# Sparse softmax in a hybrid attention block: copies of turned probabilities moved ahead of the exponentials, and the first two score products without their wait

## The chip, the cores and the metric

The kernel runs on one core of a Trainium2 chip. Its time is the device time of one execution in microseconds (us), the median of three runs. The engines are named as the profile names them: PE is TensorE (PEld its weight loads), DVE is VectorE, ACT is ScalarE, POOL is GpSimd, and SP is the queue that issues the loads.

## The reference

Two layers of a block with three attention branches over 512 positions, 8 heads each: a stick-breaking branch, a latent branch ("mla", a causal softmax), and a sparse branch ("dsa"). The change lies in the sparse branch and at the border before it. Cut to what matters:

```python
def dsa_attention(q, k, v, ix_q, ix_k, ix_w, positions, rel_bias):
    ...
    _, sel = lax.top_k(score, topk)              # 128 keys of each query
    ...
    logits = jnp.einsum('bqhd,bqkd->bqhk', qb, kg) * (dh ** -0.5)
    bias = rel_bias.astype(jnp.float32)[t5_bucket(pq[:, :, None] - pk)]
    logits = logits + jnp.moveaxis(bias, -1, 2)
    p = jax.nn.softmax(jnp.where(valid[:, :, None, :], logits, -jnp.inf), axis=-1)
    return jnp.einsum('bqhk,bqkd->bqhd', p, vg)
```

The gates, an up projection for each branch and an output projection come after the three branches, and then the next layer.

## The kernel before, in words

Each engine has one program, written by hand in the order in which the engine works through it. Engines wait for each other on counting semaphores (`wait_ge`), and a wait holds up all that stands behind it on the same engine. So two things set what runs when: the written order and the waits.

**Units and steps.** A softmax unit is one head and one tile `t` of 128 queries. Its scores are 128 x w with w = 128(t+1), since later keys are masked. There are 32 units of the mla branch (u = 0 to 31, `N_MLA` = 32) and 32 of the sparse branch (u = 32 to 63). The sparse ones are taken in pairs: step j (0 to 15, `DSA_STEPS` = 16) has the units 32+2j and 33+2j, which are two heads (o = 0, 1) at the same t = j mod 4. So the widths go 128, 256, 384, 512 and begin again, four steps make a pair of heads, and there are four such rounds.

**What a unit goes through.** In the text, S, X and so on are these operations, with the line numbers of the kernel before:
- S: PE multiplies queries and keys into one of the banks 0 to 3 (L1018, `s_of`); X: PE adds the mask to it (L1025, `chosen_of`).
- M: DVE adds the bias and takes the row maximum, into the buffer `probs[u % 4]` (L1874); N: DVE negates the maximum (L1878).
- E: ACT takes the exponentials in place, with their sum (L1435, `exp_of`).
- I: DVE inverts the sum (L1829, `inverse`); then POOL scales the row, "norm" below (L2019).
- T: PE transposes the row in t+1 pieces into one of two banks, 4 and 5 (L1037, `t_of`).
- C: ACT copies it out of the bank into `probs_dsa[u % 4]` (L1481).
- V: PE multiplies it with the values into bank 7 (L1066, `values_of`). Every fourth step ACT copies that bank out (L1441, `pair_out`).

**The order in a step j.** PE: S of both units of j, X of both, T of the units of step j-2 (`DSA_T` = 2), V of step j-3 (`DSA_AV` = 3). DVE: M and N of both units of j, then both I. ACT: E of both units of j, then C of both units of j-2. POOL follows the I.

**The waits that matter.** S(u) waits for N(u-4), since the bank is used again. M(u) waits for X(u) and for T(u-4), since `probs` has four buffers. T(u) waits for norm(u) and for C(u-2), since there are two banks. V waits for both C of its step. For the first four sparse units S waits instead for an exponential of the mla branch (L998).

**Work that goes along.** Two slabs of weights for the next stage are split in halves into a rounded part and a rest: ACT does the first behind its step 3, 5, 7 and 9 (L631), DVE the second behind its step 4, 6, 8 and 10 (L637). At j = 16 and 17 PE runs the two halves of the first projection of the next stage, `z0_0` (L736 to L738), between the last transposes. In the steps 0 to 2 the last mla units are still finished (`mla_tail`, L1053).

Of the kernel before, what the change touches and what calls it, by code (L numbers as in the profile page):

```python
# [31 lines left out]
P = 128  # L32
# [102 lines left out]
N_MLA = N_SOFT // 2  # L135
DSA_STEPS = N_MLA // 2
DSA_T, DSA_AV = 2, 3
# [52 lines left out]
def build(nc, x, positions, norm_g, w_in, q_norm_g, kv_norm_g, w_uq, w_ukv, mla_q_g, mla_k_g,  # L190
# [4 lines left out]
    with ctx:  # L195
        def signal(name):
            signals[name] = Signal(ctx.enter_context(nc.semaphore(name)), name, known, layer)
            return signals[name]
# [93 lines left out]
        soft = [soft3[:, 0, :], soft3[:, 1, :], soft3[:, 2, :], soft4[:, :]]  # L292
# [82 lines left out]
        pv_done = signal("pv_done")  # L375
# [3 lines left out]
        probs_exp = signal("probs_exp")  # L379
        row_inv = signal("row_inv")  # L380
        probs_normed = signal("probs_normed")
        probs_turned = signal("probs_turned")
        probs_t_ready = {br: signal(f"probs_t_ready_{br}") for br in ("mla", "dsa")}
# [68 lines left out]
        def dsa_units(j):  # L452

            return [(N_MLA + 2 * j + o, o, 2 * (j // ST) + o, j % ST) for o in range(2)]
# [169 lines left out]
        def split_hi(e, name, part=None):  # L624

            s, n = SLAB_NO[name], slab_size(name)
            a, b = (0, n) if part is None else (part * n // 2, (part + 1) * n // 2)
            if not part:
                e.wait_ge(*raw_in[s % RAW].at(name))
                wait_ring_slot(e, name)  # L630
            e.copy(w_hi[:, s % RING, a:b], raw[:, s % RAW, a:b]).then_inc(*hi_ready.tick(name, part or 0))  # L631
# [12 lines left out]
        def s_bank(u):  # L644
            return bank[2 + u % S_RING] if u < N_MLA else bank[(u - N_MLA) % 4]

        def t_bank(u):
            return bank[2 + S_RING + u % T_RING]

        def turned(u):  # L650

            br, h, t = soft_units[u]
            w = P * (t + 1)
            if br == "dsa":
                return probs_dsa[:, u % 4, 0:w]
            if h % 2 == 0:
                return probs_even[:, OFF[t]:OFF[t] + w]
            return probs_odd[:, (u // (2 * ST) * ST + t) % ODD, 0:w]

        def turned_before(u):  # L660

            br, h, t = soft_units[u]
            if br == "dsa":
                return u - 4 if u >= N_MLA + 4 else N_MLA - 1
            if h % 2 == 0:
                return u - ST if u >= ST else None
            n = u // (2 * ST) * ST + t - ODD
            return n // ST * 2 * ST + ST + n % ST if n >= 0 else None
# [14 lines left out]
        def _(pe):  # L683
# [30 lines left out]
            for layer.l in range(DEPTH):  # L714
# [275 lines left out]
                def s_of(u):  # L990

                    br, h, t = soft_units[u]
                    b, w = s_bank(u), P * (t + 1)
                    q = slice(t * P, (t + 1) * P)
                    if u >= N_MLA + 4:
                        pe.wait_ge(*row_max.at(u - 4))
                    elif u >= N_MLA:
                        pe.wait_ge(*probs_exp.at(N_MLA - 1 if u % 2 else N_MLA - 2))  # L998
                    elif u >= S_RING:
                        pe.wait_ge(*probs_exp.at(u - S_RING))  # L1000
                    else:
                        pe.wait_ge(*stick_prob.at(N_STICK - 1))
                    if br == "mla":
                        if t == 0:


                            pe.wait_ge(*dve_evac.at(f"qh{h}rope"))
                            pe.wait_ge(*pool_work.at(f"kh{h}rope"))
                            pe.wait_ge(*dve_evac.at(f"kh{h}"))
                        pe.matmul(b[:, 0:w], q_head[:, h % 2, q], k_head[:, h % 2, 0:w], start=True, stop=True)  # L1010
                        mm = pe.matmul(b[:, w - P:w], big_eye[:, :], causal[:, :], start=False, stop=True, skip_group_check=True)
                        mm.then_inc(*logits.tick(u))
                    else:
                        if h == 0 and t == 0:
                            pe.wait_ge(*dve_evac.at("ds_q3"))
                            pe.wait_ge(*topk.at("chosen", ST - 1))
                        r = slice(HD * (h % 2), HD * (h % 2) + HD)
                        pe.matmul(b[:, 0:w], ds_q[r, h // 2, q], ds_k[r, 0:w], start=True, stop=True)  # L1018
# [59 lines left out]
                for i in range(N_MLA):  # L1078
                    s_of(i)
                    if i in (1, 2):  # L1080
                        values_b(i + 1)
                    br, h, t = soft_units[i]
                    if h + 1 < HEADS:
                        if t == 0:
                            prep_k(h + 1)
                        if t == 2 and h + 2 < HEADS:
                            prep_q(h + 2)
                    if i >= T_LAG:
                        t_of(i - T_LAG)
                    if h + 1 < HEADS:  # L1090
                        if i == 0:
                            norm_q(1)
                        if t == 1:
                            norm_k(h + 1)
                        if t == 3 and h + 2 < HEADS:
                            norm_q(h + 2)
                    if i >= AV_LAG and soft_units[i - AV_LAG][1] % 2:
                        av_of(i - AV_LAG)
# [77 lines left out]
        def _(e):  # L1176
# [66 lines left out]
            for layer.l in range(DEPTH):  # L1243
# [184 lines left out]
                def exp_of(u):  # L1428
                    br, h, t = soft_units[u]
                    w = P * (t + 1)  # L1430
                    e.wait_ge(*row_max.at(u))
                    if br == "mla" and u >= PR:
                        e.wait_ge(*probs_turned.at(u - PR))
                    dst = probs[:, u % PR, 0:w]
                    e.activation(dst, s_bank(u)[:, 0:w] if br == "mla" else dst, ACT.Exp, bias=stat[:, 16 + u % 4:17 + u % 4],  # L1435
                                 accum_out=stat[:, 20 + u % 4:21 + u % 4]).then_inc(*probs_exp.tick(u))

                def pair_out(br, pair, u):

                    e.wait_ge(*pv_done.at("soft", u))  # L1440
                    e.copy(y[:, 4 + pair, :] if br == "mla" else y_dsa[:, pair, :], bank[Y][:, :]).then_inc(*y_out[br].tick(pair))  # L1441

                for i in range(N_MLA):
                    if i > AV_LAG and (i - AV_LAG - 1) % 8 == 7:
                        pair_out("mla", (i - AV_LAG - 1) // 8, i - AV_LAG - 1)
                    br, h, t = soft_units[i]
# [21 lines left out]
                for j in range(DSA_STEPS + DSA_AV + 1):  # L1468
                    if j >= DSA_AV + ST and (j - DSA_AV) % ST == 0:
                        pair = (j - DSA_AV) // ST - 1  # L1470
                        pair_out("dsa", pair, N_MLA + 8 * pair + 7)
                    if j < DSA_STEPS:
                        for u, o, h, t in dsa_units(j):
                            exp_of(u)
                    if N_MLA + 2 * j - AV_LAG == N_MLA - 1 or N_MLA + 2 * j + 1 - AV_LAG == N_MLA - 1:
                        pair_out("mla", 3, N_MLA - 1)
                    if 0 <= j - DSA_T < DSA_STEPS:
                        for u, o, h, t in dsa_units(j - DSA_T):
                            e.wait_ge(*probs_turned.at(u))
                            e.wait_ge(*pv_done.at("soft", turned_before(u)))  # L1480
                            e.copy(turned(u), t_bank(u)[:, 0:P * (t + 1)]).then_inc(*probs_t_ready["dsa"].tick(u))  # L1481
                    if j in SPLIT_Z:
                        split_hi(e, *SPLIT_Z[j])

# [572 lines left out]
```

## Time and profile before

| | |
|---|---|
| runs, us | 1379.31, 1379.43, 1378.16; median 1379.31 |
| the profiled execution | 1379.81 us, of which the span of the trace is 1378.1 us |
| PE busy | 1287.8 us (93%) |
| DVE busy | 775.8 us (56%) |
| ACT busy | 608.3 us (44%) |
| sparse steps of layer 0 | PE from 358.46 us, `z0_0` begins at 414.23 us |
| sparse steps of layer 1 | PE from 1007.59 us, `z0_0` begins at 1064.00 us |
| mean granted clock of TensorE | 0.981 of full speed |

A row of the timeline gives the start, the duration, the engine, the line and operation, what is written and read, and in brackets the idle time of the engine just before and who ended it. "x2" is two instructions that follow each other. PE's clock in the views of windows is the share of full speed that was granted: 1.00 is 2.4 GHz, 0.50 is 1.2 GHz.

### The profile page before, as it was taken

What the parts mean: (1) busy time and instruction counts of PE and PEld (TensorE: products, weight loads), DVE (VectorE), ACT (ScalarE), POOL (GpSimd) and SP (SyncE); (2) the same over time, 40 slices, a digit from 0 to 9 for tenths busy, and PEclk for the clock granted to TensorE, in tenths of its full rate; (3) what the DMA queues carried; (4) which work ended last, traced back from release to release, by engine and by line L of the source; (5) the groups of instructions that cost most, each with busy time, mean ns of one, the idle gap of its engine ahead of it and who ended that gap; (6) DMA issues with size and microseconds to landing.
All of it is one profiled execution on the core that took longest, in us unless ns stands there. A gap on an engine that the chain in (4) does not pass through costs nothing.

```text
span 1378.1 us, 17854 instructions
## 1 busy us (share of the span) xinstructions
PE 1287.8 (93%) x6530; PEld 971.6 (71%) x6538; DVE 775.8 (56%) x1582; ACT 608.3 (44%) x1130; POOL 181.3 (13%) x302
## 2 busy tenths in 40 slices
PE   3589999999889999999999999999988999999998
PEld 2277767656558888888888776665555888888887
DVE  7956577778653333354436667777855323435442
ACT  3335456666564223223324455666656322323330
POOL 3400111123330000000000021112333000000000
PEclk9899999999989999999999999999999999999999
DMA  6432221110241322222332311110024133232321
GB/s 167 115 115 84 70 62 32 46 31 1 81 135 31 122 92 92 92 92 92 101 83 92 93 62 62 33 54 22 17 74 126 50 104 92 92 95 90 121 93 61
DMA packets 118424, 109.15 MB, mean 79 GB/s; under 512 B 34496, under 2 KB 101056, under 8 KB 118336
## 3 DMA queue, kind: packets, MB, share of 16 engines
q1 hardware_dynamic: 110096, 107.96, 26.1%
q10 hardware_dynamic: 8240, 0.03, 0.3%
q8 instruction: 53, 0.87, 0.3%
q14 instruction: 35, 0.29, 0.1%
HBM read 100.64 MB, written 7.34 MB: 78 GB/s over the span
## 4 chain that ended last, share of the span: by engine, by line
PE 74%; DVE 10%; ACT 7%; issue 5%; POOL 2%; SPq 1%; DMA 0%; DVEq 0%; ACTq 0%
PE bank L736 19%; PE bank L738 19%; PE bank L737 19%; PE bank L844 2%; PE bank L1037 2%; PE bank L1010 2%; PE bank L1053 2%; DVE probs L1874 1%; POOL reach L466 1%; PE bank L868 1%; DVE w_lo L637 1%; ACT soft L1333 1%; PE bank L1066 1%; ACT soft L1335 1%; PE bank L885 1%
## 5 line engine op out<-in xcount | busy, mean ns | idle before, releaser
L736 PE MATMUL bank<-h_hi,w_hi 128*128 128x512 f32 (+1 forms) x928 | 360.1, 388 | 3.6 <-DVE h_lo L1567 2.2
L738 PE MATMUL bank<-h_hi,w_lo 128*128 128x512 f32 (+1 forms) x928 | 352.7, 380 | 0.0
L737 PE MATMUL bank<-h_lo,w_hi 128*128 128x512 f32 (+1 forms) x928 | 352.6, 380 | 0.0
L637 DVE TENSOR_TENSOR w_lo<-raw,w_hi 128x2048 fp32r<-128x2048 f32 (+2 forms) x98 | 187.7, 1916 | 129.0 <-ACT w_hi L631 128.9
L631 ACT CAST w_hi<-raw 128x2048 fp32r<-128x2048 f32 (+2 forms) x100 | 159.3, 1595 | 118.7 <-PE bank L738 118.7
L736 PEld LDWEIGHTS bank<-h_hi,w_hi 128*128 128x128 f32 x928 | 175.7, 189 | 46.9 <-issue 9.4
L738 PEld LDWEIGHTS bank<-h_hi,w_lo 128*128 128x128 f32 x928 | 175.7, 189 | 33.5
L737 PEld LDWEIGHTS bank<-h_lo,w_hi 128*128 128x128 f32 x928 | 175.7, 189 | 32.5 <-issue 1.9
L1508 ACT ACTIVATE gate<-bank,gains 128x512 f32<-128x512 f32 x48 | 33.0, 688 | 166.1 <-PE bank L738 166.1
L2019 POOL TENSOR_SCALAR probs<-probs,stat 128x128 f32<-128x128 f32 (+3 forms) x128 | 75.4, 590 | 167.7 <-DVE stat L1829 162.1
L1037 PE MATMUL bank<-mats,probs 128*128 128x128 f32 x320 | 57.7, 298 | 18.3 <-ACT probs_dsa L1481 18.3
L736 PE MATMUL bank<-br_hi,w_hi 128*128 128x512 f32 x192 | 74.7, 389 | 0.0
L737 PE MATMUL bank<-br_lo,w_hi 128*128 128x512 f32 x192 | 74.7, 389 | 0.0
L738 PE MATMUL bank<-br_hi,w_lo 128*128 128x512 f32 x192 | 74.7, 389 | 0.0
L1923 DVE TENSOR_TENSOR gate<-gate,bank 128x512 f32<-128x512 f32 x32 | 22.0, 686 | 84.8 <-PE bank L738 84.8
L694 PE MATMUL bank<-reach,step_w 128*32 128x128 f32 (+3 forms) x256 | 33.8, 492 | 38.1 <-DVE reach L466 25.9
L1037 PEld LDWEIGHTS bank<-mats,probs 128*128 128x128 f32 x320 | 42.3, 154 | 36.9 <-POOL probs L2019 22.6
L1435 ACT ACTIVATE probs<-probs,stat 128x128 f32<-128x128 f32 (+3 forms) x64 | 35.9, 562 | 44.4 <-DVE stat L1878 41.2
L694 PEld LDWEIGHTS bank<-reach,step_w 128*32 128x32 f32 x256 | 15.7, 118 | 55.3 <-issue 27.9
L1333 ACT ACTIVATE soft<-soft 128x128 f32<-128x128 f32 (+3 forms) x64 | 29.6, 463 | 56.4 <-DVE soft L1737 56.4
L1435 ACT ACTIVATE probs<-bank,stat 128x128 f32<-128x128 f32 (+1 forms) x64 | 33.4, 522 | 42.7 <-DVE stat L1846 42.7
L1703 DVE MATCH_REPLACE8 score<-stat,score 128x256 f32<-128x256 f32 (+2 forms) x96 | 51.6, 540 | 0.0
(221 smaller groups left out, 2184.9 us busy)
## 6 DMA issues: line engine op xcount, KB each, us to landing
raw<-in_w_in SPq DMA_DIRECT2D x56, 1024.0 KB, 5.2
raw<-in_w_branch SPq DMA_DIRECT2D x12, 1024.0 KB, 5.1
raw<-in_w_out SPq DMA_DIRECT2D x8, 1024.0 KB, 5.1
bias<-bias_dram SPq DMA_DIRECT2D x16, 256.0 KB, 3.0
bias<-bias_dram SPq DMA_DIRECT2D x16, 192.0 KB, 2.6
x_sb<-in_x SPq DMA_DIRECT2D x4, 512.0 KB, 5.1
bias_dram<-bias_out SPq DMA_DIRECT2D x8, 256.0 KB, 2.9
raw<-in_w_in SPq DMA_DIRECT2D x4, 512.0 KB, 4.6
```

The costliest lines, as they stand in the source:

```text
L631: e.copy(w_hi[:, s % RING, a:b], raw[:, s % RAW, a:b]).then_inc(*hi_ready.tick(name, part or 0))
L637: e.tensor_tensor(w_lo[:, s % RING, a:b], raw[:, s % RAW, a:b], w_hi[:, s % RING, a:b].bitcast(F32), ALU.subtract).then_inc(*lo_signal(nam ...
L694: mm = pe.matmul(bank[G % 8][32 * g4:32 * g4 + 32, 0:w], step_f[:, 0:32], reach[:, g % 8, 0:w], start=True, stop=True)
L736: pe.matmul(out_ap, lh, rh, start=start and i == 0, stop=False)
L737: pe.matmul(out_ap, lh, rl, start=False, stop=False)
L738: mm = pe.matmul(out_ap, ll, rh, start=False, stop=stop and i == n - 1)
L1037: mm = pe.transpose(t_bank(u)[:, k * P:(k + 1) * P], probs[:, u % PR, k * P:(k + 1) * P], eye)
L1333: e.activation(v, v, ACT.Exp).then_inc(*stick_exp.tick("exp", u))
L1435: e.activation(dst, s_bank(u)[:, 0:w] if br == "mla" else dst, ACT.Exp, bias=stat[:, 16 + u % 4:17 + u % 4], accum_out=stat[:, 20 + u % 4: ...
L1508: e.activation(gate[:, m, :], dbank(f"g{n}_{mm}")[:, :], ACT.Sigmoid, bias=gain[:, N_GAINS + g:N_GAINS + 1 + g]).then_inc(*gate_sig.tick(f ...
L1703: e.match_replace(row, best, row, TAKEN).then_inc(*topk.tick("replace", rnd, t))
L2019: e.tensor_scalar(probs[:, u % PR, 0:w], probs[:, u % PR, 0:w], stat[:, 24 + u % 4:25 + u % 4], 1.0, ALU.mult, ALU.mult).then_inc(*probs_n ...
```

## The change

There are two edits. First, S of the first two sparse units no longer waits for the last two exponentials of the mla branch; it writes banks 0 and 1, which those exponentials do not read. The next two units (banks 2 and 3) keep the wait. Second, ACT takes C of step j-2 ahead of E of step j, from j = 3 on. At j = 2 the copies stay behind the exponentials and the `pair_out` of the mla branch. PE, DVE, POOL and SP keep their order.

```diff
@@ -994,8 +994,10 @@
                     if u >= N_MLA + 4:
                         pe.wait_ge(*row_max.at(u - 4))
+                    elif u >= N_MLA + 2:
+                        pe.wait_ge(*probs_exp.at(N_MLA - 1 if u % 2 else N_MLA - 2))
                     elif u >= N_MLA:
-                        pe.wait_ge(*probs_exp.at(N_MLA - 1 if u % 2 else N_MLA - 2))
+                        pass
@@ -1469,16 +1471,22 @@
+                    def turned_dsa():
+
+                        for u, o, h, t in dsa_units(j - DSA_T):
+                            e.wait_ge(*probs_turned.at(u))
+                            e.wait_ge(*pv_done.at("soft", turned_before(u)))
+                            e.copy(turned(u), t_bank(u)[:, 0:P * (t + 1)]).then_inc(*probs_t_ready["dsa"].tick(u))
+
+                    if DSA_AV <= j < DSA_STEPS + DSA_T:
+                        turned_dsa()
                     if j < DSA_STEPS:
                         for u, o, h, t in dsa_units(j):
                             exp_of(u)
                     if N_MLA + 2 * j - AV_LAG == N_MLA - 1 or N_MLA + 2 * j + 1 - AV_LAG == N_MLA - 1:
                         pair_out("mla", 3, N_MLA - 1)
-                    if 0 <= j - DSA_T < DSA_STEPS:
-                        for u, o, h, t in dsa_units(j - DSA_T):
-                            e.wait_ge(*probs_turned.at(u))
-                            e.wait_ge(*pv_done.at("soft", turned_before(u)))
-                            e.copy(turned(u), t_bank(u)[:, 0:P * (t + 1)]).then_inc(*probs_t_ready["dsa"].tick(u))
+                    if j == DSA_T:
+                        turned_dsa()
```

ACT's order in the steps 2 to 6, first before the change. `probs<-probs` is E, `probs_dsa<-bank` is C, `w_hi<-raw` is the split, `y<-bank` the `pair_out` of the mla branch:

```order
L1435 ACTIVATE probs,stat<-probs,stat 128x384 x2
L1441 COPY y<-bank 128x512
L1481 COPY probs_dsa<-bank 128x128 x2
L1435 ACTIVATE probs,stat<-probs,stat 128x512 x2
L1481 COPY probs_dsa<-bank 128x256 x2
L631 CAST w_hi<-raw 128x1024
L1435 ACTIVATE probs,stat<-probs,stat 128x128 x2
L1481 COPY probs_dsa<-bank 128x384 x2
L1435 ACTIVATE probs,stat<-probs,stat 128x256 x2
```

And the same place in the changed kernel:

```order
L1437 ACTIVATE probs,stat<-probs,stat 128x384 x2
L1443 COPY y<-bank 128x512
L1479 COPY probs_dsa<-bank 128x128 x2
L1479 COPY probs_dsa<-bank 128x256 x2
L1437 ACTIVATE probs,stat<-probs,stat 128x512 x2
L631 CAST w_hi<-raw 128x1024
L1479 COPY probs_dsa<-bank 128x384 x2
L1437 ACTIVATE probs,stat<-probs,stat 128x128 x2
L1479 COPY probs_dsa<-bank 128x512 x2
L1437 ACTIVATE probs,stat<-probs,stat 128x256 x2
```

From the second pair of copies on, each has moved ahead of one pair of exponentials, and the split stands directly behind the exponentials.

PE's order at the border between the branches, before, with the semaphores that each row waits for. The first rows are the last transposes of unit 28 and then S and X of the units 32 and 33; what follows are the transposes of unit 29 and 30:

```order
L1037 MATMUL bank<-mats,probs 128x128 [waits probs_t_ready_mla,probs_normed]
L1018 MATMUL bank<-ds_k,ds_q 128x128 [waits topk,dve_evac,probs_exp]
L1018 MATMUL bank<-ds_k,ds_q 128x128 [waits probs_exp]
L1025 MATMUL bank<-causal,big_eye 128x128 x2
L1037 MATMUL bank<-mats,probs 128x128 [waits probs_t_ready_mla,probs_normed]
L1037 MATMUL bank<-mats,probs 128x128
```

And in the changed kernel:

```order
L1039 MATMUL bank<-mats,probs 128x128 [waits probs_t_ready_mla,probs_normed]
L1020 MATMUL bank<-ds_k,ds_q 128x128 [waits topk,dve_evac]
L1020 MATMUL bank<-ds_k,ds_q 128x128
L1027 MATMUL bank<-causal,big_eye 128x128 x2
L1039 MATMUL bank<-mats,probs 128x128 [waits probs_t_ready_mla,probs_normed]
L1039 MATMUL bank<-mats,probs 128x128
```

Nothing has moved there; both waits for `probs_exp` are gone.

## Rows read from the trace of the kernel before

**Rows 1.** The page: the clock in 40 slices, and the chain that ended last.

```profile
PEclk9899999999989999999999999999999999999999
...
PE 74%; DVE 10%; ACT 7%; issue 5%; POOL 2%; SPq 1%; DMA 0%; DVEq 0%; ACTq 0%
```

**Rows 2.** Windows: length, PE, PEld, DVE, ACT, POOL busy, clock, DMA, GB/s.

```profile
370.83:413.89 43.06, 35.27 (x252) 22.24 (x254) 23.27 (x101) 28.54 (x79) 16.33 (x24) 0.84 0.41 123
1019.96:1063.66 43.70, 35.35 (x252) 22.05 (x254) 23.31 (x101) 28.53 (x79) 16.33 (x24) 0.84 0.41 121
```

**Rows 3.** Waits, 1005 to 1076 us: who for whom, total, times, longest.

```profile
DVE probs L1874 <- PE bank L1037: 14.8, 15, 2.3
PEld bank L1037 <- POOL probs L2019: 11.5, 9, 2.7
PE bank L1037 <- ACT probs_dsa L1481: 9.4, 9, 2.6
```

**Rows 4.** Timeline, layer 1: from T of step 5 to T of step 6.

```profile
1034.31 0.60 PE L1037 MATMUL bank<-mats,probs 128*128 128x128 f32 x4
...
1038.03 0.62 ACT L1481 COPY probs_dsa<-bank 128x256 f32<-128x256 f32 x2
...
1038.53 0.85 PE L1037 MATMUL bank<-mats,probs 128*128 128x128 f32 x6 [2.60 <-ACT probs_dsa L1481]
```

**Rows 5.** Timeline of DVE: first M and last I of the steps 11 to 14.

```profile
1049.69 0.68 DVE L1874 CUSTOM_DVE_ANT_0 probs<-bank,bias 128x512 f32<-128x512 f32 x1
...
1052.40 0.16 DVE L1829 RECIPROCAL stat<-stat 128x1 f32<-128x1 f32 x1 [0.79 <-POOL probs L2019]
1053.60 0.29 DVE L1874 CUSTOM_DVE_ANT_0 probs<-bank,bias 128x128 f32<-128x128 f32 x1 [1.03 <-PE bank L1037]
...
1055.29 0.16 DVE L1829 RECIPROCAL stat<-stat 128x1 f32<-128x1 f32 x1 [0.47 <-POOL probs L2019]
1057.30 0.42 DVE L1874 CUSTOM_DVE_ANT_0 probs<-bank,bias 128x256 f32<-128x256 f32 x1 [1.84 <-PE bank L1037]
...
1059.27 0.16 DVE L1829 RECIPROCAL stat<-stat 128x1 f32<-128x1 f32 x1 [0.52 <-ACT probs L1435]
1060.33 0.56 DVE L1874 CUSTOM_DVE_ANT_0 probs<-bank,bias 128x384 f32<-128x384 f32 x1 [0.90 <-PE bank L1037]
...
1062.68 0.16 DVE L1829 RECIPROCAL stat<-stat 128x1 f32<-128x1 f32 x1 [0.65 <-ACT probs L1435]
```

**Rows 6.** Timeline of ACT: a half of a split, and copy pairs of three widths.

```profile
1045.89 1.05 ACT L631 CAST w_hi<-raw 128x1024 fp32r<-128x1024 f32 x1
...
1055.17 0.84 ACT L1481 COPY probs_dsa<-bank 128x384 f32<-128x384 f32 x2
...
1059.15 1.05 ACT L1481 COPY probs_dsa<-bank 128x512 f32<-128x512 f32 x2
...
1062.55 0.41 ACT L1481 COPY probs_dsa<-bank 128x128 f32<-128x128 f32 x2
```

**Rows 7.** Groups by shape, 1009.29 to 1076 us: the rest of the split on DVE.

```profile
L637 DVE TENSOR_TENSOR w_lo<-raw,w_hi 128x1024 fp32r<-128x1024 f32 x4 | 4.8, 1205 | 0.0
```

**Rows 8.** Timeline, layer 1, the border: S and T on PE, a norm on POOL.

```profile
1007.59 0.49 PE L1018 MATMUL bank<-ds_k,ds_q 64*128 64x128 f32 x2
1009.29 0.48 PE L1018 MATMUL bank<-ds_k,ds_q 64*128 64x128 f32 x2 [1.21 <-ACT probs L1435]
...
1009.83 0.71 PE L1037 MATMUL bank<-mats,probs 128*128 128x128 f32 x5
...
1008.59 0.58 POOL L2019 TENSOR_SCALAR probs<-probs,stat 128x384 f32<-128x384 f32 x1 [1.02 <-DVE stat L1829]
```

**Rows 9.** Windows of the half-clock stretches of layer 1 (columns as in rows 2).

```profile
1022.35:1029.05 6.70, 6.00 (x30) 4.32 (x32) 3.03 (x13) 3.56 (x12) 2.66 (x4) 0.50 0.29 95
1039.32:1042.40 3.08, 3.08 (x18) 2.04 (x18) 2.26 (x9) 2.01 (x7) 1.64 (x2) 0.51 0.23 73
1053.00:1056.20 3.20, 3.20 (x18) 1.90 (x17) 1.16 (x8) 1.73 (x6) 1.10 (x3) 0.50 1.00 342
```

## The prediction, made before the changed kernel ran

> **What bounds the kernel now.** I read the page first. The chain that ended last is PE for 74% [rows 1], and outside three places the granted clock is nearly full. So most of the kernel is a line of matrix products that this change does not touch, and it can only pay where PE stands still. The slices of PE's clock that show 8 lie in the sparse steps of the two layers, so I read the windows next: from M of step 3 to M of step 15 the sparse stage takes 43.06 us in layer 0 and 43.70 us in layer 1, with PE busy for 35.3 us at a mean clock of 0.84 [rows 2]. Then the waits: PE stands 9.4 us for the copies C, nine times, up to 2.6 us, and DVE's M stands 14.8 us for PE; PE's weight loads are put down to POOL's norms for 11.5 us [rows 3]. The timeline shows how these hang together. T of step 5 begins at 1034.31, so the bank is ready to be copied at about 1034.9. C of step 5 starts at 1038.03, since it stands behind both E of step 7, and T of step 6, which needs the bank back, starts at 1038.53 after 2.60 us of standing still [rows 4]. So there is a round trip through the exponentials in every step: T(j-2), M(j), E(j), C(j-2), T(j-1). E(j) itself cannot be earlier than T(j-2), because M(j) writes the buffer that T(j-2) reads.
>
> The idle time also costs clock. In layer 1 the clock is at 0.50 to 0.51 (the level of 1.2 GHz) for 6.70, 3.08 and 3.20 us [rows 9], 13.0 us together; each stretch comes after PE had waited for copies (the second begins less than a microsecond after the wait that ended at 1038.53).
>
> **First edit: the two scores.** S of unit 33 was issued at 1009.29 after a wait of 1.21 us, while S of unit 32 was done with at about 1008.0 [rows 8]. Behind it stand both X, T of unit 29 (two transposes), T of unit 30 (three), and all later work of PE. Without the wait, S and X go through by about 1008.3 and T of unit 29 follows. T of unit 30 then waits for its norm, which ends at 1008.59 + 0.58 = 1009.17 [rows 8], and starts at about 1009.2. Before, it started two transposes of 0.11 us after 1009.83, at 1010.05. So PE gains 0.83 us, and as it works without a pause from there to T of step 0, the gain is carried into the first M that waits for a T. Nothing is added. The bounds are 0.5 us (DVE's first M can't start before the last mla reciprocal ends at about 1009.43, where it started at 1009.97) and the whole 1.21 us. I take 0.83 us a layer.
>
> **Second edit: the copies.** No instruction is added or removed. C(j-2) now takes place while DVE does M(j), for which ACT had to wait anyway. What is then late next? PE is not: over the twelve steps it was busy 35.35 us, of which 12.3 us at half clock [rows 2, 9] are 6.1 us of full-clock work, so it has 29.2 us of work, 9.7 us for four steps. The longer line is that of DVE and ACT, which alternate: M, M, E, I, then the next M. Its length is in the steps 11 to 14, from the first M to the end of the last I [rows 5]:
> - width 512: 1052.40 + 0.16 - 1049.69 = 2.87
> - width 128: 1055.29 + 0.16 - 1053.60 = 1.85
> - width 256: 1059.27 + 0.16 - 1057.30 = 2.13
> - width 384: 1062.68 + 0.16 - 1060.33 = 2.51
>
> That is 9.36 us for four steps and 28.1 us for the twelve steps 3 to 14. Added to it:
> - the rest of the split on DVE behind four of the steps, 1.2 us each [rows 7]: 4.8 us.
> - what ACT comes late by. Between its last E and the next it has the copies, and DVE has I, M and N, which take about 0.7 us at width 128, 0.8 at 256 and 1.0 at 384. In steps 4 and 8 ACT has a split half (1.05) and the pair of width 384 (0.84) [rows 6], 1.2 us more than DVE needs, of which I take 1.1, as E and M of the second unit are a little apart. In steps 6 and 10 it is 1.05 + 0.41 - 1.0, 0.4 us. In step 12 0.84 - 0.7 and in step 13 1.05 - 0.8 [rows 6], together 0.3 us with the slack. In steps 5 and 9 DVE is busy with the split, which hides the copies. Together 2.2 + 0.8 + 0.3 = 3.3 us.
>
> The sum is 36.2 us from M(3) to M(15). Against 43.70 and 43.06 us [rows 2] this is 7.5 and 6.9 us less. The wait of T of step 1 for C of step 0 stays, since that copy isn't moved. Behind step 15 nothing changes: PE goes from `z0_0` to the last V without a pause, before and after. Then the next projection follows on PE, so the gain is carried to the end.
>
> **The clock.** The 36.2 us are with PE at full clock. It will still stand: I expect 1 to 1.7 us before T of steps 3, 6, 7 and 10, where DVE and ACT do the split as well. That is shorter and rarer than now, but the clock may still fall once in a layer. A stretch of 3.2 us at half clock takes 1.6 us of PE's time. In the first eight steps it disappears in the 3 us and more by which four steps of DVE with splits are longer than PE's 9.7; in the last four, 9.36 against 9.7, it counts in full. I take the middle, 0.8 us a layer. By the Trainium skill ("TensorE: Matmul & The Clock Gate", section Terms) the penalty is the time at the lower clock times one half, which for the 13.0 us of layer 1 [rows 9] would be 6.5 us. No row here shows that the path pays all of that now; by that rule an edit that leaves the stretches where they are would save far less than my sum, which is the first rival below.
>
> **The sum.** 7.5 + 6.9 + 2 x 0.83 - 2 x 0.8 = 14.5 us. The profiled execution had 1379.81 us (span 1378.1), 0.5 above the median of 1379.31. So I expect a median of 1364.8 us and a span of about 1363.6.
>
> **The rivals.**
> - *The stretches at half clock stay, or PE waits for the norms instead.* For it: T of a step needs the norm as well as the copy, and PE's loads are put down to POOL [rows 3]; 13 us at half clock hold 6.5 us of lost work. Against: in [rows 4] norm of step 6 had long ended. If half of the gain of the second edit is lost, 14.4 x 0.5 + 1.7 gives 8.9 us: 1370.4 us. Chance 0.14.
> - *The copies take the place of the exponentials* (slower). If C(j-2) starts only when M(j) has ended, because T of the second unit comes late, each E comes a pair of copies later. The pairs of four steps are 0.41, 0.62, 0.84 and 1.05 us [rows 4, 6], 2.9 us, so twelve steps have 8.8 us on the line; with the splits on ACT, 4 x 1.05, it is 28.1 + 4.8 + 8.8 + 4.2 = 45.9 us, 2.2 more than the 43.70 of now. Less the first edit that is 1.4 us a layer: 1382.1 us. It decides once more than 7.5 us of the copies' and splits' 13.0 are not hidden. Against it: M waits for the same T as C, so both start together. Chance 0.03.
> - *PE stays at half clock through the stage* (slower). PE's 29.2 us of work takes 29.2 + h/2 with h us at half clock, and passes 43.7 us when h is over 29; all of it gives 58.4 us, 14 us more per layer, 1408 us. A busier PE speaks against it. Chance 0.01.
> - *Nothing*: a wait that I don't see, such as the loads of the bias, sets the steps, and only the first edit or not even that shows: 1377.6 to 1379.3 us. Bias loads are issued four steps ahead of their use, and no M is put down to one. Chance 0.04.
> - *More than I say*: the clock stays full and DVE's line is the whole: 14.4 + 2 x 1.2 gives 16.8 us, 1362.5. It is in my case's range. The forecast, with its spread from 1361 to 1367.5, has the chance 0.78.
>
> The range of 8 in 10 reaches from 1361 to the rival of half the gain, 1371. About 0.2% (2.8 us) is what a measurement of this kernel can tell from no change. Faster by more than that 0.93, within it 0.04, slower 0.03.
>
> **What would show it.** In the profile after, the sparse window from M(3) to M(15) is 35 to 38 us in both layers. PE's waits for `probs_dsa` fall from 9.4 to about 2 to 3 us, what is left being step 1's, and waits for norms or for N take a part of it. S of unit 33 follows S of unit 32 without a pause. C of step 5 stands before E of step 7 in time. The clock in the window is 0.92 or more instead of 0.84. The forecast is wrong if the clock stays at 0.84, if ACT's E waits for T rather than for N, or if PE's work after the stage starts no earlier relative to the start of the layer.

## The result and the profile after

The changed kernel takes 1360.13 us (median of 5 runs, 1357.4 to 1362.37) against 1379.31 us before. The ratio is 0.9866, with a 95% interval from 0.9855 to 0.9877. That is 19.2 us less, where 14.5 were forecast; the time is just outside the range, at its fast end. The profiled execution has a span of 1358.1 us against 1378.1.

The page of the changed kernel, its PE line, the clock in 40 slices and the chain:

```profile
PE 1277.5 (94%) x6538; PEld 964.8 (71%) x6538; DVE 776.5 (57%) x1582; ACT 607.4 (45%) x1130; POOL 181.5 (13%) x302
...
PEclk9899999999999999999999999999999999999999
...
PE 74%; DVE 9%; ACT 8%; issue 5%; POOL 2%; SPq 1%; DMA 0%; ACTq 0%; DVEq 0%
```

Next to [rows 1] the shares of DVE and ACT have moved by one per cent and PE's has not. Of the two slices with an 8, the one in the sparse steps of layer 0 (379 to 413 us) is full; the other (34 to 69 us) lies ahead of the stage and stays. The slices of layer 1's sparse steps showed a 9 before as well. The windows from M of step 3 to M of step 15, the counterpart of [rows 2], and a stretch within the first of them:

```profile
369.65:403.64 33.99, 31.08 (x253) 19.56 (x252) 23.52 (x101) 27.96 (x80) 15.96 (x24) 0.95 0.49 144
1009.19:1043.52 34.33, 30.10 (x253) 18.48 (x252) 23.49 (x100) 27.83 (x80) 15.95 (x24) 1.00 0.49 146
370.43:373.72 3.29, 3.29 (x24) 2.42 (x20) 2.13 (x12) 3.02 (x7) 1.39 (x2) 0.53 0.53 141
```

The windows are 9.1 and 9.4 us shorter, and the clock is at 0.95 and 1.00 where it was at 0.84. The waits of layer 1, for [rows 3], from 995 to 1056 us, which begins and ends at about the same places of the program:

```profile
ACT probs L1437 <- DVE stat L1886: 11.0, 11, 3.1
...
PEld bank L1039 <- POOL probs L2027: 6.2, 5, 2.0
PE bank L1039 <- ACT probs_dsa L1479: 4.0, 4, 1.6
DVE probs L1882 <- PE bank L1039: 3.9, 4, 2.1
```

PE waits 4.0 us for copies instead of 9.4, M 3.9 us for PE instead of 14.8. The place of [rows 4] in the timeline, layer 1: T of step 5, C of step 5, T of step 6, E of step 7:

```profile
1019.15 0.60 PE L1039 MATMUL bank<-mats,probs 128*128 128x128 f32 x4
...
1020.47 0.65 ACT L1479 COPY probs_dsa<-bank 128x256 f32<-128x256 f32 x2
...
1021.58 0.89 PE L1039 MATMUL bank<-mats,probs 128*128 128x128 f32 x6
...
1022.25 0.72 ACT L1437 ACTIVATE probs<-probs,stat 128x512 f32<-128x512 f32 x1 [1.13 <-DVE stat L1886]
```

From T of step 5 to T of step 6 it is 2.43 us instead of 4.22, and T of step 6 has no wait in front of it. C is done before E of step 7 begins.

The whole stage, from the last exponential of the mla branch to the table load behind the stage, went from 65.61 to 56.03 us in layer 0 and from 66.20 to 56.37 in layer 1: 9.58 + 9.83 = 19.4 us. The other 0.6 us between the spans lie outside (0.5 of it ahead of the sparse steps of layer 0), in code that is the same.

### The profile page after: what moved, and what is told of

Read it like the earlier page. It is cut to its first block, busy times and chain, and to the rows that moved or that the text cites. A ratio compares the mean times of both kernels' runs of the same rounds, so it can differ in the third digit from the quotient of the medians.

```text
span 1358.1 us, 17862 instructions
## 1 busy us (share of the span) xinstructions
PE 1277.5 (94%) x6538; PEld 964.8 (71%) x6538; DVE 776.5 (57%) x1582; ACT 607.4 (45%) x1130; POOL 181.5 (13%) x302
## 4 chain that ended last, share of the span: by engine, by line
PE 74%; DVE 9%; ACT 8%; issue 5%; POOL 2%; SPq 1%; DMA 0%; ACTq 0%; DVEq 0%
PE bank L736 20%; PE bank L738 19%; PE bank L737 19%; PE bank L844 3%; PE bank L1012 2%; PE bank L1039 2%; PE bank L1055 2%; PE bank L868 1%; POOL reach L466 1%; ACT w_hi L631 1%; ACT soft L1335 1%; ACT soft L1337 1%; PE bank L885 1%; DVE w_lo L637 1%; DVE probs L1882 1%
## 5 line engine op out<-in xcount | busy, mean ns | idle before, releaser
L1039 PE MATMUL bank<-mats,probs 128*128 128x128 f32 x320 | 52.5, 279 | 8.5 <-ACT probs_dsa L1479 7.0
L1039 PEld LDWEIGHTS bank<-mats,probs 128*128 128x128 f32 x320 | 37.6, 142 | 26.2 <-POOL probs L2027 11.6
L1997 POOL TENSOR_SCALAR_AFFINE_SELECT soft<-soft 128x128 f32<-128x128 f32 x64 | 23.9, 377 | 209.1 <-DVE soft L1753 208.8
```

The costliest lines, as they stand in the source:

```text
L1039: mm = pe.transpose(t_bank(u)[:, k * P:(k + 1) * P], probs[:, u % PR, k * P:(k + 1) * P], eye)
```

## Experiments

The kernel before was timed anew beside each group of runs, and a run's time is compared with that. In the table, "before" is this time, "border" is the time from the start of the last mla exponential to M of step 3, "window" that from M of step 3 to M of step 15 (layer 0, layer 1), and the clock that of the window.

| run | time, us | before, us | border | window | clock |
|---|---|---|---|---|---|
| before | 1379.31 | | 11.51, 11.50 | 43.06, 43.70 | 0.84, 0.84 |
| changed | 1360.13 | 1379.31 | 10.86, 10.85 | 33.99, 34.33 | 0.95, 1.00 |
| scores alone | 1377.88 | 1377.66 | 10.85, 10.85 | 43.22, 43.58 | 0.84, 0.84 |
| copies alone | 1361.60 | 1377.66 | 11.51, 11.51 | 33.99, 34.35 | 1.00, 1.00 |
| before, filled | 1371.06 | 1377.66 | 11.51, 11.51 | 39.48, 39.83 | 1.00, 1.00 |
| first copy ahead as well | 1356.64 | 1377.66 | 9.74, 9.73 | 33.98, 34.32 | 1.00, 1.00 |
| VectorE's split cut | 1351.23 (one run) | 1378.10 | 10.86, 10.85 | 30.75, 31.09 | 1.00, 1.00 |
| ScalarE's split cut | 1356.75 (one run) | 1378.10 | 10.86, 10.85 | 32.63, 32.99 | 1.00, 1.00 |
| splits moved, first copy ahead | 1352.94 | 1378.10 | 10.73, 10.72 | 32.18, 31.81 | 1.00, 1.00 |

### The first scores alone

```diff
+                    elif u >= N_MLA + 2:
+                        pe.wait_ge(*probs_exp.at(N_MLA - 1 if u % 2 else N_MLA - 2))
                     elif u >= N_MLA:
-                        pe.wait_ge(*probs_exp.at(N_MLA - 1 if u % 2 else N_MLA - 2))
+                        pass
```

> The first edit alone on the kernel before (the first two score products without their wait; the copies stay behind the exponentials). In the profile of the changed kernel the stretch from the last exponential of the mla branch to M of step 3 was 10.86 us instead of 11.51 in both layers, 0.65 us less. If that is the first edit's and adds to the rest, this run has the same 10.86 us, M of step 3 to M of step 15 stays at 43 to 43.7 us, and the time is 1.3 us below the kernel before, about 0.999 of it. Rival: the 0.65 us come from the other edit or are taken back in the next wait for a copy; then the stretch is 11.5 us and the time is the same.

The time against the kernel before on the same chip is 1.0002 (0.9993 to 1.0011). The interval holds no change and reaches down to 1.0 us less; the 1.3 us that were expected lie just outside it, so in the time the first edit is not seen, and its share of the gain rests on the profiles. In the profile it is: the border is 10.85 us in both layers, that of the changed kernel, and the two windows together are 86.80 us where they were 86.76, at the same clock:

```profile
370.13:413.35 43.22, 35.70 (x255) 22.04 (x254) 23.24 (x101) 28.55 (x79) 16.37 (x24) 0.84 0.40 123
1019.01:1062.59 43.58, 35.83 (x255) 22.14 (x254) 23.29 (x100) 28.55 (x79) 16.40 (x24) 0.84 0.41 121
```

### The copies alone

The second part of the diff without the first.

> The second edit alone (the copies ahead of the exponentials from step 3 on; the first scores wait as before). If the edits add up, M of step 3 to M of step 15 is 34.0 to 34.3 us in both layers as in the changed kernel, the stretch before it is 11.5 us, and the time is 1.3 us above the changed kernel, about 1361.5 us. Rival: the two edits need each other; then the stretch from M of step 3 to M of step 15 is 36 us or more.

The time is 1361.60 us, ratio 0.9882 (0.9865 to 0.9899). Windows:

```profile
369.36:403.35 33.99, 29.75 (x253) 18.41 (x252) 23.48 (x101) 27.88 (x80) 16.03 (x24) 1.00 0.49 148
1011.34:1045.69 34.35, 30.11 (x253) 18.48 (x252) 23.50 (x101) 27.88 (x80) 16.02 (x24) 1.00 0.49 151
```

The window is that of the changed kernel to 0.02 us, and the border that of the kernel before. So in the profiles the edits add up, and nearly all of the gain is the copies'. In the times, this run is 16.1 us below the kernel before beside it, and the changed kernel 19.2; the intervals overlap, and a difference of 1.3 us can't be read from them. This run also has no stretch at half clock in layer 0, where the changed kernel's profile has one of 3.29 us, and the window is 33.99 us in both: that stretch cost nothing.

It has another one outside the stage, where the changed kernel has none:

```profile
932.20:935.60 3.40, 3.40 (x8) 1.73 (x7) 1.22 (x4) 1.87 (x4) 0.00 (x0) 0.51 0.01 2
```

From the table load behind the stage of layer 0 to the last mla exponential of layer 1 it is 585.30 us here and 583.52 in the changed kernel, 1.8 more. ScalarE's timelines of the two run alike up to this stretch and drift apart within 5 us of its start.

### The kernel before with its waits filled

```diff
                         for u, o, h, t in dsa_units(j):
                             chosen_of(u)
+                        if j >= 3 and j % 4 in (0, 3):
+                            for _k in range(6 if j % 4 == 0 else 4 if j == 3 else 0):
+                                pe.matmul(bank[NORM][:, :], h_hi[:, 0, 0:P], h_hi[:, 0, :], start=True, stop=True)
```

> The kernel before with products added that nobody reads, in a bank that is free in this stage: six of 128x512 (about 0.23 us each) on TensorE ahead of the transposes of the steps 4, 8 and 12 and four in step 3, where TensorE waits 1.6 to 2.6 us for copies. They are to keep the clock up and change no wait. Theory A (a good part of the second edit's gain is the clock): the clock in the window from M of step 3 to M of step 15 goes from 0.84 to 1.00, and the window from 43.7 to about 39.5 us, some 8 us over both layers, 1371 us. Theory B (the waits are all, half clock costs the path less than 1 us a layer): the clock goes up and the window stays at 42.5 to 43.7 us.

The time is 1371.06 us, ratio 0.9952 (0.9939 to 0.9966): a kernel that does more work in the same order is 6.6 us faster. Windows, and PE's timeline where the added products stand in a wait (its first row shows five of the six):

```profile
369.99:409.47 39.48, 34.91 (x273) 21.10 (x272) 23.51 (x100) 28.57 (x79) 16.39 (x24) 1.00 0.45 134
1015.56:1055.39 39.83, 34.92 (x273) 21.10 (x272) 23.48 (x100) 28.57 (x79) 16.38 (x24) 1.00 0.45 134
```

```profile
1016.73 1.32 PE L1108 MATMUL bank<-h_hi 128*128 128x512 f32 x5
1018.65 0.85 PE L1037 MATMUL bank<-mats,probs 128*128 128x128 f32 x6 [0.60 <-ACT probs_dsa L1484]
```

Theory A holds; the two windows are 7.5 us shorter together. At full clock the old order takes 39.5 and 39.8 us, 3.6 and 3.9 less than with 13 us at half clock. So of the 9.1 and 9.4 us that the copies bring in the window, 3.6 and 3.9 are the clock that no longer falls, and 5.5 are what the order brings with the clock full in both (39.48 - 33.99, 39.83 - 34.33).

### The first copies ahead as well

```diff
-                    if DSA_AV <= j < DSA_STEPS + DSA_T:
+                    if DSA_T <= j < DSA_STEPS + DSA_T:
                         turned_dsa()
...
-                    if j == DSA_T:
-                        turned_dsa()
```

> The changed kernel, and also in step 2 the copies of step 0 stand ahead of the exponentials and of the mla branch's last copy out. In the changed kernel TensorE still waits 1.56 us there. If the round trip through the exponentials is what makes each step late, M of step 2 to M of step 3 falls from 3.68 us to about 2.7, the clock no longer drops behind it, and the time is about 2 us below the changed kernel (1358). Rival: the copies push the exponentials of step 2 back by 0.4 us and the norm becomes what the transposes wait for; then nothing is gained.

The time is 1356.64 us, ratio to the kernel before 0.9854 (0.9839 to 0.9869). That is 21.0 us below the kernel before beside it, 1.8 more than the changed kernel gains, where about 2 were expected. M of step 2 to M of step 3 falls from 3.68 to 2.56 us in both layers, and the border with it from 10.86 to 9.74. The wait that the changed kernel left standing was the same round trip, and could be had as well. The window behind it is unchanged:

```profile
366.54:400.52 33.98, 29.77 (x252) 18.48 (x252) 23.49 (x100) 28.10 (x81) 16.53 (x25) 1.00 0.52 151
1005.01:1039.33 34.32, 30.12 (x252) 18.52 (x252) 23.48 (x100) 28.10 (x81) 16.54 (x25) 1.00 0.51 155
```

### VectorE's part of the splits cut

In this run and the next the weights of `z0` are partly not split, so the next stage computes with other numbers.

```diff
             a, b = (0, n) if part is None else (part * n // 2, (part + 1) * n // 2)
+            if part is not None and name.startswith("z0"):
+                b = a + 32
             e.wait_ge(*hi_ready.at(name, part or 0))
```

> The changed kernel, and VectorE's part of the four split halves in the sparse stage is cut from 1024 to 32 columns (so the first projections of the next stage read wrong rests; ScalarE's part is whole). It tells what VectorE's part costs. If its 1.2 us stand in the line in full, M of step 3 to M of step 15 falls from 34.0 to about 29.5 us. By the terms of my prediction it would be 36.2 - 4.8, and the copies of the steps 5 and 9 no longer hidden, 31.9. Rival: TensorE's own 9.7 us for four steps take over and the window stays above 30.5 us.

```profile
367.33:398.08 30.75, 28.58 (x250) 17.98 (x252) 19.64 (x101) 27.92 (x80) 12.40 (x24) 1.00 0.55 164
1003.79:1034.88 31.09, 28.50 (x250) 17.95 (x252) 19.61 (x100) 27.95 (x80) 12.40 (x24) 1.00 0.56 162
```

The window falls by 3.24 us in both layers. Of the three numbers, 29.5 and 31.9 are wrong, and "above 30.5" holds, though not for the reason given: TensorE's 9.7 us do not set these steps, since the steps 3 to 6 and 7 to 10 take 10.5 us each. DVE's part stands between its second I and the next M, and the 32 columns that are left still take 0.15 us there. The steps 6 and 8 of layer 0 fall by 1.0 us each, which is the whole of the rest. Its steps 4 and 10 fall by 0.7 and 0.6 only, since something else comes in ahead of the next M: 0.29 us of idle time in step 4 for which the profile names nobody, and in step 10 a wait for PE (in layer 1 the steps 6 and 10 have it). Layer 0, step 10:

```profile
387.80 0.16 DVE L1839 RECIPROCAL stat<-stat 128x1 f32<-128x1 f32 x1 [0.53 <-ACT probs L1439]
387.88 0.17 DVE L639 TENSOR_TENSOR w_lo<-raw,w_hi 128x32 fp32r<-128x32 f32 x1
388.38 0.69 DVE L1884 CUSTOM_DVE_ANT_0 probs<-bank,bias 128x512 f32<-128x512 f32 x1 [0.33 <-PE bank L1041]
```

The second I of step 10 starts 2.35 us after its M (385.45), as it does in the changed kernel, so ScalarE is not late there in either.

### ScalarE's part of the splits cut

The same cut, in `split_hi`.

> The changed kernel, and ScalarE's part of the four split halves in the sparse stage is cut from 1024 to 32 columns (the next stage reads stale weights; VectorE's part is whole). It tells how late ScalarE's split makes the exponentials. By the term of my prediction (1.1 us in the steps 4 and 8, 0.4 us in 6 and 10) the window from M of step 3 to M of step 15 would fall by 3.0 us less the 0.15 us that a copy pair alone is late. By the step times of the changed kernel (3.48 us in steps 4 and 8, where 1.82 + 1.2 would be 3.02; 3.55 in 6 and 10, where 2.51 + 1.2 would be 3.71) it falls by 0.9 us, to 33.1 us, all of it in the steps 4 and 8.

```profile
368.97:401.60 32.63, 29.30 (x250) 18.38 (x252) 23.37 (x100) 25.03 (x80) 15.98 (x24) 1.00 0.53 157
1007.43:1040.42 32.99, 29.64 (x250) 18.44 (x252) 23.35 (x100) 25.03 (x80) 15.97 (x24) 1.00 0.53 156
```

The window falls by 1.36 and 1.34 us: more than the 0.9 that the changed kernel's step times had let me expect, and less than half of the 3.0 by the prediction's term. All of it is in steps 4 and 8, which go from 3.48 to 2.80 us, 0.68 each. The steps 6 and 10 stay at 3.55. ScalarE's timeline of this run, layer 0, steps 3 and 4:

```profile
370.85 0.72 ACT L1439 ACTIVATE probs<-probs,stat 128x512 f32<-128x512 f32 x1
371.47 0.18 ACT L1439 ACTIVATION_READ_ACCUMULATOR probs<-probs,stat 128x1 f32 x1
371.57 0.20 ACT L633 CAST w_hi<-raw 128x32 fp32r<-128x32 f32 x1
371.67 0.85 ACT L1481 COPY probs_dsa<-bank 128x384 f32<-128x384 f32 x2
372.43 0.40 ACT L1439 ACTIVATE probs<-probs,stat 128x128 f32<-128x128 f32 x1
```

And the same place in the changed kernel, ACT and DVE together:

```profile
372.24 1.03 ACT L631 CAST w_hi<-raw 128x1024 fp32r<-128x1024 f32 x1
372.37 0.16 DVE L1837 RECIPROCAL stat<-stat 128x1 f32<-128x1 f32 x1 [0.78 <-POOL probs L2027]
372.59 0.29 DVE L1882 CUSTOM_DVE_ANT_0 probs<-bank,bias 128x128 f32<-128x128 f32 x1
...
373.18 0.85 ACT L1479 COPY probs_dsa<-bank 128x384 f32<-128x384 f32 x2
...
373.92 0.41 ACT L1437 ACTIVATE probs<-probs,stat 128x128 f32<-128x128 f32 x1
...
374.83 0.16 DVE L1837 RECIPROCAL stat<-stat 128x1 f32<-128x1 f32 x1 [0.22 <-ACT probs L1437]
...
374.91 1.23 DVE L637 TENSOR_TENSOR w_lo<-raw,w_hi 128x1024 fp32r<-128x1024 f32 x1
...
376.07 0.41 DVE L1882 CUSTOM_DVE_ANT_0 probs<-bank,bias 128x256 f32<-128x256 f32 x1
```

The second I of step 4 starts 2.24 us after M of that step; in step 12, which has the same width and no split of ACT's before it, it is 1.60, and in step 4 of the run with the cast cut 1.59. So the cast makes it 0.65 us late. The rows also show the seams between instructions. The cast is shown with 1.03 us, but the copies start 0.94 us after it; the copies are shown with 0.85, and E starts 0.74 after them. DVE's split part is shown with 1.23, and the next M starts 1.16 after it. So each of these three has a shown duration that reaches 0.07 to 0.11 us into the next instruction, and a sum of shown durations is too long at such a seam.

### The splits moved, with the first copies ahead

```diff
-SPLIT_Z = {3: ("z0_0", 0), 5: ("z0_0", 1), 7: ("z0_1", 0), 9: ("z0_1", 1)}
+SPLIT_Z = {1: ("z0_0", 0), 5: ("z0_0", 1), 9: ("z0_1", 0), 13: ("z0_1", 1)}
```

> The kernel with the first copies ahead as well (e4), and the four split halves moved from ScalarE's steps 3, 5, 7, 9 to 1, 5, 9, 13, where a step of width 384 follows, in which VectorE needs longest in relation to the copies. If ScalarE's lateness in the steps 4 and 8 is 0.45 us each, that goes, and one of VectorE's parts (1.2 us) moves into step 2, where it waits for a transpose: the window from M of step 3 to M of step 15 falls from 34.0 to 31.9 us if step 2 takes it up for nothing, 2 us a layer and 4 us in all, 1352.5 us. Rival: the last round of four steps is bound by TensorE (9.7 us), or the later second slab makes the loads of the next stage late; then it is the same as e4 or slower.

The time is 1352.94 us, ratio 0.9819 (0.9805 to 0.9832). It gains 25.2 us on the kernel before beside it, where the first copies ahead alone gain 21.0 and the changed kernel 19.2. This is the fastest version with the whole computation. Windows:

```profile
368.43:400.61 32.18, 29.89 (x250) 18.63 (x251) 22.43 (x101) 27.33 (x78) 15.53 (x25) 1.00 0.45 135
1007.02:1038.83 31.81, 30.23 (x250) 18.70 (x251) 22.46 (x100) 27.15 (x78) 15.52 (x25) 1.00 0.44 135
```

The steps 4 and 8 take 1.8 to 2.2 us instead of 3.5. The part that went to step 2 was not for nothing: that step is 3.55 us again instead of 2.56. The one that went to step 14 costs 0.8 us there (3.55 instead of 2.75), and from M of step 15 to the table load it is 10.39 us instead of 11.20, so that this much comes back. From the last mla exponential to the table load the stage is 53.30 and 52.92 us, against 54.92 and 55.25 with the first copies ahead, 4.0 us less together.

## Why the prediction was right and wrong

**The mechanism was right, and two terms of its sum were not.** The round trip T, M, E, C, T set the steps, the copies left it, and the line of DVE and ACT took over. The gain is carried to the end: from the table load behind the stage of layer 1 it is 303.41 us before and after. Each rival that ends at no change or slower is out: copies and exponentials do not pile up, and PE's clock rises. Half of the gain was not lost either.

**The first edit** was worth 0.65 us in both layers, where I had said 0.83. The wait for the norm of unit 30 is as forecast. PE's timeline of the changed kernel shows it (the last mla exponential starts at 998.34):

```profile
997.43 0.49 PE L1020 MATMUL bank<-ds_k,ds_q 64*128 64x128 f32 x4
997.86 0.28 PE L1027 MATMUL bank<-causal,big_eye 128*128 128x128 bf16 x2
997.98 0.39 PE L1039 MATMUL bank<-mats,probs 128*128 128x128 f32 x2
999.11 0.55 PE L1039 MATMUL bank<-mats,probs 128*128 128x128 f32 x3 [0.74 <-POOL probs L2027]
...
1000.90 0.63 PE L1039 MATMUL bank<-mats,probs 128*128 128x128 f32 x4
```

T of unit 30 starts 0.77 us after that exponential and did so 1.59 us after it before [rows 8], 0.82 less. The next transposes start 2.56 us after it and 3.24 before, 0.68 less: there 0.14 us go to something else. In the program they wait for DVE's copy of unit 29, which stands behind DVE's first two M, and the first M starts 1.52 us after the exponential before and 1.03 after, only 0.5 less. That this is the cause was not tried alone, and the profile shows no idle time of PE in front of that row.

**The step that failed is the sum of 36.2 us for the line of DVE and ACT**, above all its term "what ACT comes late by", 3.3 us. The line measured 34.0 and 34.3 us, and cutting ScalarE's splits shows 1.4 us for that term. Step by step, in layer 0:
- steps 3, 7, 11: 2.94, 2.93 and 2.94 against 2.87 each. Right.
- steps 5, 9, 13: 2.18, 2.18 and 2.19 against 2.13 (2.28 in step 13). Right.
- steps 4 and 8: 3.48 against 1.85 + 1.2 + 1.1 = 4.15. The cut of ScalarE's part shows 0.68 us of lateness in place of 1.1. The rest is mostly the seams: without that part a step with VectorE's split takes 2.80, not 3.05.
- step 12: 1.81 against about 2.0.
- steps 6 and 10: 3.55 against 2.51 + 1.2 + 0.4 = 4.11. ScalarE's lateness of 0.4 is nothing here: cutting its part changes nothing in these steps. The rest, 0.16, is the seams.
- step 14: 2.76 against 2.51, where PE is the longer line.

In layer 1 step 7 takes 3.29 us, with 0.41 us of idle time ahead of its second M that the profile puts down to PE; why only there is not shown.

So the term for ACT was 1.9 us too long, which is about the whole miss of 2.2 and 1.9 us. Shown durations added end to end made the sum another 0.8 us or so too long, and steps that came out longer than their term, most of all step 14, took 0.6 of it back in layer 0 and 0.9 in layer 1.

**The clock.** I had set 0.8 us a layer against the gain, for one stretch at half clock. One profile has such a stretch in layer 0, of 3.29 us, and it cost nothing. It lies in the steps 3 and 4, where the prediction's own argument has it vanish; none fell in the last four steps, so what it would cost there was not seen. The two errors, about 2 us and 0.8 us a layer, less 0.2 for the first edit and 0.2 behind M of step 15, are the 4.9 us between 14.5 and the 19.4 of the stage. Both had the same sign, and the range went only 3.8 us beyond the forecast to the fast side, since I had put all the doubt on the slow side.

**The rule of the Trainium skill** ("TensorE: Matmul & The Clock Gate", section Terms) prices the time at the lower clock at one half: 6.5 us for the 13.0 us of layer 1. The filled kernel shows 3.9 us. The measurement decides: in this stage, where other engines set part of the time, the penalty is about 0.3 us for each microsecond at half clock, and it was nothing for the stretch in the steps 3 and 4 of the changed kernel. The stretch outside the stage in the run with the copies alone cost 1.8 us for its 3.4, about the page's half. The prediction left open what the path pays for the clock. Its sum did not need this share, as it added the new line from its parts, but a reader of it would have put the whole gain down to the order of the copies, and 40% of it is the clock.

**What the profile was to show.** The window of 35 to 38 us was missed from below. The clock of 0.92 or more holds. PE's waits for copies are 4.0 us instead of 2 to 3: besides the 1.57 us before T of step 1 there are 0.88, 1.23 and 0.28 us before T of the steps 3, 7 and 11, where C of the step before stands behind ACT's work, in the steps 3 and 7 behind a split. The first of them (the row is PE's, layer 1):

```profile
1013.33 1.07 PE L1039 MATMUL bank<-mats,probs 128*128 128x128 f32 x8 [0.88 <-ACT probs_dsa L1479]
```

**Slips in the prediction that the result does not rest on.** Only one of the slices with an 8 lies in the sparse steps (layer 0); for layer 1 the low clock is seen in the windows alone. The rival of the copies in the place of the exponentials passes the 43.70 us of now only when 10.8 of the 13.0 us are not hidden (43.7 - 28.1 - 4.8), not 7.5. And the two rivals that end slower have 0.04 together, where the last line gives 0.03.

## What to carry to other kernels

On an engine that works in order, an instruction that others wait for should stand ahead of one that is late anyway: look for a copy that frees a bank and is queued behind work which depends on the same producer. Where a matrix engine waits in short pieces, its clock may be a part of the loss, and independent products put into the wait tell that part before anything is reordered. When a line of work is added up from a trace, add distances from start to start and not shown durations, and leave room on the fast side as well.

## What the runs showed of the hardware

More work made the kernel faster: the added products, some 22 of 128x512 in each layer, raised the clock in the window from 0.84 to 1.00 and took 6.6 us off the time, with every semaphore wait of the program as it was. And the clock's stretches are not the same from run to run: with the same code in the window, layer 0 had one of 3.29 us in the profile of the changed kernel and none in that of the copies alone. What a stretch costs depends on where it lies: that one cost nothing, 13.0 us of them in the old order cost 3.9, and 3.4 us between the stages, in the run with the copies alone, cost 1.8.
